# Expert-choice tail: all five chunks summed in PSUM with split one-hot products, and stores that add to a pre-filled output

## What is computed

```python
def expert_choice_ffn(h, w_router, w_gate_up, w_down):
    cap = CAP_FACTOR * N // N_EXPERTS
    aff = jax.nn.softmax((h @ w_router).astype(jnp.float32), axis=-1)
    g, idx = lax.top_k(jnp.swapaxes(aff, 1, 2), cap)
    xs = jax.vmap(lambda hb, ib: hb[ib])(h, idx)
    gu = jnp.einsum('becd,edf->becf', xs, w_gate_up)
    gate, up = jnp.split(gu, 2, axis=-1)
    y = jnp.einsum('becf,efd->becd', jax.nn.silu(gate) * up, w_down) * g[..., None].astype(h.dtype)
    return jax.vmap(lambda ib, yb: jnp.zeros((N, D), yb.dtype).at[ib.reshape(-1)].add(yb.reshape(-1, D)))(idx, y)
...
    ff = expert_choice_ffn(modulate(x, shift2, scale2), w_router, w_gate_up, w_down)
    x = layer_norm(ALPHA * x + gate2 * ff, ln2_g, ln2_b)
```

## Time and profile before

| what | us |
|---|---|
| median of the runs | 950.67 |
| the profiled execution, its own time | 954.81 |
| its span | 953.0 |
| TensorE busy | 880.7 (92%) |
| VectorE busy | 772.8 (81%) |
| ScalarE busy | 574.2 (60%) |
| GpSimd busy | 158.0 (17%) |
| DMA, mean over the span | 285 GB/s |

### The profile page before, as it was taken

How to read it: one execution, slowest core, us unless ns; L and a number is a source line. 1 busy time by engine, 2 the same in 40 slices (tenths; PEclk the granted TensorE clock), 3 DMA queues, 4 the chain that set the end, 5 groups by cost and what they waited for, 6 DMA issues and landing times.

```text
span 953.0 us, 11594 instructions
## 1 busy us (share of the span) xinstructions
PE 880.7 (92%) x4615; PEld 600.9 (63%) x4615; DVE 772.8 (81%) x797; ACT 574.2 (60%) x588; POOL 158.0 (17%) x105
## 2 busy tenths in 40 slices
PE   2899999899999966999999999999999999999982
PEld 0389978256678843666666666666666666666651
DVE  2777736678779876889988988998998998999857
ACT  1345266735751343776776777777777777777732
POOL 1000300110011024103203303302321330320210
PEclk9899999989999986999999999999999999999996
DMA  8920500753048296999999999999999999999525
GB/s 282 396 119 1 205 1 1 291 128 114 2 169 329 100 366 263 355 419 389 416 393 391 411 390 389 400 396 379 384 413 383 379 403 392 372 398 375 181 58 190
DMA packets 57165, 272.08 MB, mean 285 GB/s; under 512 B 6772, under 2 KB 7016, under 8 KB 40728
## 3 DMA queue, kind: packets, MB, share of 16 engines
q1 hardware_dynamic: 48552, 243.81, 65.7%
q0 software_dynamic: 7120, 22.29, 8.5%
q10 hardware_dynamic: 1440, 5.24, 1.4%
HBM read 258.05 MB, written 13.28 MB: 285 GB/s over the span
## 4 chain that ended last, share of the span: by engine, by line
PE 85%; DVE 7%; DMA 4%; ACT 2%; issue 1%; SPq 0%; POOL 0%; DVEq 0%; ACTq 0%
PE PS L903 24%; PE PS L904 24%; PE PS L905 24%; DMA ring<-in_w_mod 3%; PE PS L1067 2%; PE PS L1051 1%; PE PS L918 1%; PE PS L1021 1%; PE PS L1090 1%; PE PS L1222 1%; PE PS L1209 1%; PE PS L1145 1%; DVE xf L1799 1%; DVE smin L1536 1%; ACT prob L710 1%
## 5 line engine op out<-in xcount | busy, mean ns | idle before, releaser
L1716 DVE TENSOR_TENSOR Wl<-wr,Wh 128x2048 fp32r<-128x2048 f32 x190 | 432.6, 2290 | 51.3 <-ACT Wh L821 51.3
L821 ACT ACTIVATE Wh<-wr 128x2048 fp32r<-128x2048 f32 x192 | 367.4, 1915 | 69.1 <-PE PS L905 69.0
L903 PE MATMUL PS<-Wh,Xh 128*80 128x512 f32 x512 | 203.1, 397 | 1.5 <-DVE Xl L1721 0.8
L905 PE MATMUL PS<-Wl,Xh 128*80 128x512 f32 x512 | 201.5, 394 | 0.0
L904 PE MATMUL PS<-Wh,Xl 128*80 128x512 f32 x512 | 201.4, 393 | 0.0
L538 POOL DMA_INDIRECT acc_scratch<-ysc,idx_u x16 | 81.0, 5062 | 428.4 <-DVE ysc L1747 418.7
L905 PEld LDWEIGHTS PS<-Wl,Xh 128*80 128x80 f32 x512 | 76.0, 148 | 42.4 <-issue 0.5
L903 PEld LDWEIGHTS PS<-Wh,Xh 128*80 128x80 f32 x512 | 76.0, 148 | 42.1 <-issue 1.6
L903 PE MATMUL PS<-Wh,HTh 128*80 128x512 f32 x256 | 101.6, 397 | 0.0
L904 PEld LDWEIGHTS PS<-Wh,Xl 128*80 128x80 f32 x512 | 76.1, 149 | 39.5 <-issue 0.4
L904 PE MATMUL PS<-Wh,HTl 128*80 128x512 f32 x256 | 100.4, 392 | 0.0
(11 more groups left out here) (288 smaller groups left out, 1193.6 us busy)
## 6 DMA issues: line engine op xcount, KB each, us to landing
wr<-in_w_gate_up SPq DMA_DIRECT2D x128, 1024.0 KB, 10.1
wr<-in_w_down SPq DMA_DIRECT2D x64, 1024.0 KB, 9.4
ring<-in_w_mod SPq DMA_DIRECT2D x24, 1024.0 KB, 8.9
xt<-in_x_sample ACTq DMA_DIRECT2D x8, 512.0 KB, 7.8
ring<-in_w_in SPq DMA_DIRECT2D x4, 1024.0 KB, 13.4
ring<-in_w_out SPq DMA_DIRECT2D x4, 1024.0 KB, 10.7
w_qkv<-in_w_in SPq DMA_DIRECT2D x4, 768.0 KB, 10.2
h_scratch<-h POOLq DMA_DIRECT2D x5, 512.0 KB, 4.8
```

Of the source, the lines that this page charges most:

```text
L821: act.activation(Wh[n % NWH][:], wr[s][:], ACT.Copy).then_inc(W_hi, 1)
L903: pe.matmul(out, w[0], x[0], start=first, stop=False)
L905: return pe.matmul(out, w[0], x[1], start=False, stop=last)
L1716: dve.tensor_tensor(Wl[s][:], wr[s][:], Wh[n % NWH][:].bitcast(F32), ALU.subtract).then_inc(W_lo, 1)
```

## The change

`FIN_PS` is gone; all five chunks are summed in PSUM, in the banks of `FIN_BANK`, and chunk 4 reuses chunk 0's (it waits for `z_ok`). Expert 15 isn't scattered. Its rows, and for chunk 0 also expert 14's, go through one-hot matrices in single-pass products: ScalarE rounds `ysc` to `yh`, VectorE subtracts for `yl`. Chunk 0 is loaded once scatter 13 is done, chunks 1 to 4 once scatter 14 is; scatter 14 waits until chunk 0 has been read. `FIN_ACT` is chunk 3 alone, read from PSUM. For the sample chunks VectorE makes the centring pass and the reciprocal only, ScalarE makes the multiplication (`scaled`), and the offset `ln2b` is written to all of `y_sample` during expert 3's gate/up slots by four plain stores of GpSimd, so that the last stores, now GpSimd's, add the scaled rows to it in DRAM. The prompt chunk keeps both passes on VectorE and its store on SyncE. At the start the constants' semaphore `const_in` is merged into `rows_in`, and `pads_ok` and `hout` are dropped; where ScalarE and TensorE waited for 9 of `rows_in` they wait for 10.

```diff
@@ -89,7 +89,7 @@
 W_LO_AT = {14: 0, 15: 1}
 K_OUT = (0, 1, 2, 4, 5, 6, 7, 3)
 MOD4_AT = (2, 2, 2, 2, 3, 3, 3, 3)
-FIN_PS, FIN_ACT = (0, 1), (3, 4)
+FIN_BANK, FIN_ACT = (4, 2, 6, 0, 4), 3
 OUT_ORDER = (PC,) + tuple(range(PC))
 W_POOL = 2
 N_HOLD = 8
@@ -262,7 +262,9 @@
     assert XF_SLOT + 3 <= NSLOT
     xf = at("xf", [P, CH, D], Dz + 8192 * XF_SLOT)
     iota = at("iota", [SL, NT], Fz)
-    hot = at("hot", [SL, NT], Fz + 4096)
+    hot = [at("hot0", [SL, P], Fz + 8192, F32R), at("hot1", [SL, NT], Fz + 4096, F32R)]
+    yh = [at("yh0", [SL, D], Cz + 12288, F32R), at("yh1", [SL, D], Dz + 8192 * XF_SLOT + 20480, F32R)]
+    yl = [at("yl0", [SL, D], Cz + 16384, F32R), at("yl1", [SL, D], Fz + 10752, F32R)]
     ln2g = at("ln2g", [P, D], Fz + 32768)
     ln2b = at("ln2b", [P, D], Fz + 36864)
     G2 = at("G2", [SL, D], Cz)
@@ -412,15 +415,14 @@
         sp.wait_ge(x_t, 2 * (NE - 1))
         sp.dma_start(iota[:], t["consts"][0:SL, P + 256:]).then_inc(misc_in, 16)
         sp.wait_ge(W_used, GU0[NE - 1] + 6)
-        sp.wait_ge(scattered, 16 * (NE - 1))
+        sp.wait_ge(scattered, 16 * (NE - 2))
         for c in range(CH):
-            if c == len(FIN_PS):
-                sp.wait_ge(scattered, 16 * NE)
+            if c == 1:
+                sp.wait_ge(scattered, 16 * (NE - 1))
             sp.dma_start(xf[:, c, :], acc_dram[c * P:(c + 1) * P, :]).then_inc(acc_in[c], 16)
-        for c in range(CH):
-            sp.wait_ge(y_out, c + 1)
-            sp.dma_start(y_s[:, c, :] if c < PC else t["y_prompt"][0], xf[:, c, :]).then_inc(stored, 16)
-        sp.wait_ge(stored, 16 * CH)
+        sp.wait_ge(prompt_ok, 1)
+        sp.dma_start(t["y_prompt"][0], xf[:, PC, :]).then_inc(acc_in[PC], 16)
+        sp.wait_ge(acc_in[PC], 32)
 
 
     @block.gpsimd
@@ -529,12 +531,11 @@
 
         def scatter(e):
 
-            pool.wait_ge(y_ok, e + 1 if e < NE - 1 else NE + 1)
+            pool.wait_ge(y_ok, e + 1)
             if e:
                 pool.wait_ge(scattered, 16 * e)
-            if e == NE - 1:
-                for c in FIN_PS:
-                    pool.wait_ge(acc_in[c], 16)
+            if e == NE - 2:
+                pool.wait_ge(acc_in[0], 16)
             pool.indirect_dma_start(acc_dram, bass.IndirectOffsetOnAxis(ap=idx_u[:, e:e + 1], axis=0), ysc[e % 2][:], None,
                                     compute_op=ALU.add).then_inc(scattered, 16)
 
@@ -562,10 +563,17 @@
                 gather(e + 2)
             if e:
                 scatter(e - 1)
-        scatter(NE - 1)
+            if e == 2:
+                pool.wait_ge(ln2_in, 32)
+                for c in range(PC):
+                    pool.dma_start(y_s[:, c, :], ln2b[:]).then_inc(stored, 16)
+        pool.wait_ge(stored, 16 * (2 + PC))
+        for c in range(PC):
+            pool.wait_ge(y_out, c + 1)
+            pool.dma_start(y_s[:, c, :], xf[:, c, :], accum_op=ALU.add).then_inc(stored, 16)
+        pool.wait_ge(stored, 16 * (2 + 2 * PC))
         pool.wait_ge(pool_out, 32)
-        pool.wait_ge(hout, 32)
-
+        
     def x_bank(e, h):
 
         return bank(7 if (e, h) == (0, 1) else 6, 0, 4 * SL)
@@ -872,28 +879,34 @@
             ins.then_inc(act_seq, 1)
             act.wait_ge(act_seq, steps[0])
 
-        def std3(c):
-            act.wait_ge(var3_ok, c + 1)
+        act.wait_ge(hrow_ok, rows_of(NE))
+        act.wait_ge(y_ok, NE - 1)
+        act.activation(yh[0][:], ysc[0][:], ACT.Copy).then_inc(yh_ok, 1)
+        for h in range(2):
+            act.wait_ge(y_ok, NE + h)
+            act.activation(yh[1][:, 512 * h:512 * h + 512], ysc[1][:, 512 * h:512 * h + 512], ACT.Copy).then_inc(yh_ok, 1)
+
+        def std3(c, n):
+            act.wait_ge(var3_ok, n)
             act.activation(nmr[:, c:c + 1], mv[:, c, 1:2], ACT.Sqrt, bias=epsc[:, 0:1]).then_inc(std3_ok, 1)
 
-        def row_sum(c, i):
-            act.wait_ge(acc_in[c], 16)
-            step(act.activation(xt[:, 3, :], xf[:, c, :], ACT.Copy, accum_out=fin[:, 0, i:i + 1]))
-            step(act.activation(nmr[:, c:c + 1], fin[:, 0, i:i + 1], ACT.Copy, scale=-1.0 / D))
-
-        def row_std(c, i):
-            step(act.activation(xt[:, 3, :], xf[:, c, :], ACT.Square, bias=nmr[:, c:c + 1], accum_out=fin[:, 1, i:i + 1]))
-            act.activation(fin[:, 0, i:i + 1], fin[:, 1, i:i + 1], ACT.Sqrt, bias=epsc[:, 0:1],
-                           scale=1.0 / D).then_inc(std3_ok, 1)
-
-        act.wait_ge(hrow_ok, rows_of(NE))
-        std3(0)
-        std3(1)
-        row_sum(3, 0)
-        std3(2)
-        row_std(3, 0)
-        row_sum(4, 1)
-        row_std(4, 1)
+        def scaled(c):
+            act.wait_ge(z_ok, c + 1)
+            act.activation(xf[:, c, :], xf[:, c, :], ACT.Copy, scale=rstd[:, c:c + 1]).then_inc(y_out, 1)
+
+        std3(0, 1)
+        scaled(0)
+        std3(1, 2)
+        scaled(1)
+        std3(2, 3)
+        act.wait_ge(fin_ps, 2 * FIN_ACT + 2)
+        step(act.activation(xt[:, 3, :], PS[:, 512 * FIN_BANK[FIN_ACT]:512 * FIN_BANK[FIN_ACT] + D], ACT.Copy, accum_out=fin[:, 0, 0:1]))
+        step(act.activation(nmr[:, FIN_ACT:FIN_ACT + 1], fin[:, 0, 0:1], ACT.Copy, scale=-1.0 / D))
+        step(act.activation(xt[:, 4, :], xt[:, 3, :], ACT.Square, bias=nmr[:, FIN_ACT:FIN_ACT + 1], accum_out=fin[:, 1, 0:1]))
+        act.activation(fin[:, 0, 0:1], fin[:, 1, 0:1], ACT.Sqrt, bias=epsc[:, 0:1], scale=1.0 / D).then_inc(std3_ok, 1)
+        scaled(2)
+        std3(4, 4)
+        scaled(3)
 
 
     @block.tensor
@@ -1266,15 +1278,23 @@
 
         pe.wait_ge(hrow_ok, rows_of(NE))
         pe.wait_ge(y_ok, NE - 1)
-        for c in FIN_PS:
+        pe.wait_ge(hot_ok, 2)
+        for c in range(CH):
             pe.wait_ge(acc_in[c], 16)
+            if c == PC:
+                pe.wait_ge(z_ok, 1)
+            out = [bank(FIN_BANK[c] + h) for h in range(2)]
             for h in range(2):
-                pe.matmul(bank(4 - 2 * c + h), ident, xf[:, c, 512 * h:512 * h + 512], start=True, stop=False)
+                pe.matmul(out[h], ident, xf[:, c, 512 * h:512 * h + 512], start=True, stop=False)
             if c == 0:
-                pe.wait_ge(hot_ok, 1)
+                pe.wait_ge(yl_ok, 1)
+                for h in range(2):
+                    pe.matmul(out[h], hot[0][:], yh[0][:, 512 * h:512 * h + 512], start=False, stop=False)
+                    pe.matmul(out[h], hot[0][:], yl[0][:, 512 * h:512 * h + 512], start=False, stop=False)
             for h in range(2):
-                pe.wait_ge(y_ok, NE + h)
-                pe.matmul(bank(4 - 2 * c + h), hot[:, c * P:(c + 1) * P], ysc[(NE - 1) % 2][:, 512 * h:512 * h + 512],
+                pe.wait_ge(yl_ok, 2 + h)
+                pe.matmul(out[h], hot[1][:, c * P:(c + 1) * P], yh[1][:, 512 * h:512 * h + 512], start=False, stop=False)
+                pe.matmul(out[h], hot[1][:, c * P:(c + 1) * P], yl[1][:, 512 * h:512 * h + 512],
                           start=False, stop=True).then_inc(fin_ps, 1)
 
 
@@ -1706,8 +1726,8 @@
         dve.tensor_tensor(idx_u[0:CAP_S, :], diff, ib, ALU.add).then_inc(slot_ok, 1)
         dve.tensor_tensor(g_slot[0:CAP_S, :], va, vb, ALU.max)
         dve.tensor_copy(g_slot[CAP_S:SL, :], vp)
-        dve.tensor_tensor(idx_last[0:CAP_S, :], diff[:, NE - 1:NE], ib[:, NE - 1:NE], ALU.add)
-        dve.tensor_copy(idx_last[CAP_S:SL, :], ip[:, NE - 1:NE]).then_inc(slot_ok, 1)
+        dve.tensor_tensor(idx_last[0:CAP_S, :], diff[:, NE - 2:NE], ib[:, NE - 2:NE], ALU.add)
+        dve.tensor_copy(idx_last[CAP_S:SL, :], ip[:, NE - 2:NE]).then_inc(slot_ok, 1)
 
         def split_lo_slot(n):
 
@@ -1751,7 +1771,15 @@
 
             dve.wait_ge(misc_in, 32)
             dve.wait_ge(x_t, 2 * NE)
-            dve.tensor_scalar(hot[:], iota[:], idx_last[:, 0:1], None, ALU.is_equal).then_inc(hot_ok, 1)
+            for i in range(2):
+                dve.tensor_scalar(hot[i][:], iota[:, 0:P if i == 0 else NT], idx_last[:, i:i + 1], None, ALU.is_equal).then_inc(hot_ok, 1)
+
+        def y_lo(i, h, lo, hi):
+
+            dve.wait_ge(yh_ok, i + h + 1)
+            if i == 0:
+                dve.wait_ge(ht_ps, 2 * NE)
+            dve.tensor_tensor(yl[i][:, lo:hi], ysc[i][:, lo:hi], yh[i][:, lo:hi].bitcast(F32), ALU.subtract).then_inc(yl_ok, 1)
 
         x_lo(0, 0)
         x_lo(0, 1)
@@ -1760,6 +1788,8 @@
         for n in range(W_POOL, len(ORDER) + LEAD + 3):
             if n < len(ORDER):
                 split_lo_slot(n)
+            if n == len(ORDER):
+                y_lo(0, 0, 0, D)
             for e in range(NE):
                 for h in range(2):
                     if e + 1 < NE and n == GU0[e] + X_AT[h] + LEAD:
@@ -1776,27 +1806,39 @@
 
 
         dve.wait_ge(ln2_in, 32)
-        for c in range(CH):
-            x = xf[:, c, :]
-            src = PS[:, 2048 - 1024 * c:3072 - 1024 * c] if c in FIN_PS else x
-            if c not in FIN_ACT:
-                if c not in FIN_PS:
-                    dve.wait_ge(acc_in[c], 16)
-                for h in range(2):
```

(68 more changed lines are left out.)

## The result

| | before | the change |
|---|---|---|
| median | 950.67 us | 955.28 us |
| ratio, 95% interval | | 1.0047 (1.0028 to 1.0065) |
| profiled execution: own time | 954.81 us | 955.28 us |
| its span | 953.0 us | 953.5 us |
| end of the split products | 922.30 us | 919.48 us |

The change is slower by 0.47%, 2.7 to 6.2 us by the interval. The forecast was 947.5 in a range of 943.3 to 951.0: wrong in sign and outside its range. One of the change's five executions ran at a mean granted clock of 0.62 and took 1380.85 us; the ratios leave out such slow ones, which the kernel before has too.

A forecast was written before the change was run, and what follows sets the result against it. It took the tail behind the split products as what could move, with VectorE the chain up to 949.95 us. Its terms ended the span at 949.9 against 953.0, -3.1 us off the 950.67 median: 947.5, range 943.3 to 951.0.

The forecast's parts named there:

- the 0.4: At the very end: 0.4 us from the last store's landing to the end of the span, giving 949.9.
- last landing: In the tail: the prompt's plain store lands last, at 949.5 us, behind store 3 at 948.2.
- the starved middle: Rival, around expert 4: the fill leaves TensorE standing still for up to 5.2 us; 952.7 us, chance 0.15.
- scatter 14's issue lengthened: Ahead of the tail: VectorE's subtraction delays GpSimd's descriptor writing for scatter 14 by 1.1 us, bounds 0 and 1.2.
- store 3 issued: In the tail: GpSimd's adding store of chunk 3 goes out at 941.05 us, after ScalarE scales it.
- prompt's store issued: In the tail: the prompt chunk's plain store goes out at 942.6 us, once VectorE has scaled chunk 4.
- an adding packet: In the last stores: a 4 KB packet of an adding store takes 312 to 328 ns, a plain one 160.
- an adding store alone, issue to landing: In the last stores: one adding store by itself takes 6.0 us, bounds 3.8 and 6.2.
- The fill: During expert 3: four plain stores to y_sample, 5.2 us of DMA time, costed at nothing behind a weights' lead of 10.
- The half clock: Rival, before chunk 1: TensorE falls to half clock in a 1.3 us pause, costing 3.4 us; 950.9 us, chance 0.10.
- The plain price: Rival, last stores: adding stores cost what plain ones do, so the prompt path ends it; 943.3 us, chance 0.15.
- the second rival's: Rival, last stores: adding stores run at the scatter's mean rate, 466 ns a packet, +1.3 us; 948.8 us, chance 0.12.

The follow-up runs named there:

- j: Run g with adding stores for chunks 0, 1 and 2 in place of 0 and 1: median 947.61 us, ratio 0.995 against the kernel before.
- a: The change with SyncE, not GpSimd, waiting for the landing of the adding stores: median 951.98 us, ratio 1.0008 against the kernel before.
- d: The change without the four plain stores that write ln2b to y_sample during expert 3: median 955.26 us, ratio 1.0034 against the kernel before.
- c: The change with GpSimd's last four stores plain, so the offset is left out: median 952.89 us, ratio 1.0012 against the kernel before.
- e: Run a with VectorE's subtraction for expert 14's low part moved behind expert 15's evacuation: median 952.69 us, ratio 1.001 against the kernel before.
- h: Run g with VectorE's subtraction for expert 14's low part moved behind expert 15's evacuation: median 944.78 us, ratio 0.9928 against the kernel before.
- g: Run f with fill and adding stores for chunks 0 and 1 only, SyncE waiting for every landing: median 945.21 us, ratio 0.9938 against the kernel before.
- i: Run a with plain stores in place of adding ones, so the offset is left out: median 948.91 us, ratio 0.9961 against the kernel before.
- b: The kernel before, with GpSimd also waiting at its end for SyncE's five plain stores: median 959.3 us, ratio 1.0074.
- f: The change without fill and adding stores; VectorE makes both passes for all five chunks, SyncE stores them: median 947.33 us, ratio 0.9952 against the kernel before.

## Why the prediction was wrong

**The step that failed** is the last one of the sum: "With the 0.4 between the last landing (949.98 + 2.6) and the end that is 949.9". I took the 0.4 from a program in which SyncE was the last to wait and carried it into one in which GpSimd is. Measured in its place: 0.2 from GpSimd's last landing, 945.3, to the drain, 7.7 of drain, 0.2 to the end. The prediction went through the release of every store and never asked which engine stands last in line and what it still has to do. The evidence was in the trace of before, as a record of 8.64 us behind GpSimd's last instruction, in no view of busy time. No rival named it; the starved middle, the only one on the slow side, was another mechanism.

**The rest of the sum held.** Measured from the end of the split products:

| step | predicted | measured |
|---|---|---|
| scatter 14's issue lengthened | 1.1 | 1.35 (5.00 against 3.65) |
| first load to landing | 4.02 | 3.3 |
| store 3 issued | 18.75 | 18.45 |
| prompt's store issued | 20.3 | 19.57 |
| an adding packet | 312 to 328 ns | 333 to 338 ns |
| an adding store alone, issue to landing | 6.0 | 5.3 (j, chunk 2) |
| last landing | 27.2 | 25.8 to 26.1 |
| landing to end of span | 0.4 | 7.9 |

The last landing is 25.8 us for GpSimd's stores and 26.1 for the prompt's, 1.1 us early, and what follows it is 7.5 too long: together the 6.4 us that were to be found. With 0.4 in the last row the tail would have been 26.5 us, 4.2 under before. No run shows that with all four adding stores. In the nearest, a, SyncE has seen every landing 26.1 us behind the split products, but the drain, begun at the last issue, ends 3.7 us later.

**The fill** was rightly costed at nothing (d), but of the lead of "10" us that was to hide it, 3.6 remain. Each of its four issues took 1.05 to 1.12 us, not 0.55. Its rival was right about the crowding; those 3.6 us kept it from deciding.

**The half clock** was rightly kept as a rival: it did not occur in the change's profile, with a pause of 0.6 us on TensorE, and did in c's with one of 2.3. What it costs the median can't be told from zero (a against e).

**The descriptors.** VectorE's subtraction has both inputs in SBUF and writes SBUF; moving it away shortened the scatter's issue by 1.1 us, from 5.00 to 3.86 (e, and h against g). The Trainium skill, page SBUF — State Buffer, section SBUF: two separate sides, infers that such an instruction spares descriptor writing. Here it does not, and the measurement decides.

**The plain price** (15%) is out: the packets cost double a plain one's 160 ns. The Trainium skill, page DMA: Bandwidth & Descriptors, section on the anatomy of a GpSimd DMA, fits 2.0 us plus bytes over 436 GB/s, by which I had estimated 3.2 us for such a store. An adding store alone took 5.3 (j), and the change's last one 7.4, issued 1.5 us behind another; a plain one issued so took 3.0 (i). The prediction calls the end by this estimate "the second rival's"; it is that of the first, the plain price. And the 3.8 us that it took as the least for a plain store were no bound.

## What to carry to other kernels

Ask of every edit which engine makes the last wait of the program and what it has to do after it: here one wait for landings on GpSimd, in addition to SyncE's, cost 7 to 8 us in a kernel where nothing else changed (b). Let SyncE wait for the landings at the end, and give GpSimd its last store some 9.3 us before the end, 11.6 with two adding ones 1.5 us apart; behind a long issue, as of a scatter, 7.3 us count from where the issue ends (f). A change of two halves is to be timed in halves: the sums in PSUM were worth 4.2 us (f), the adding stores perhaps 2.1 more for the first two chunks (g), and with all four the gain was gone (a, 1.0008 against f's 0.9952).

## What the runs showed of the hardware

GpSimd's drain at the end of its program, 7.2 to 7.7 us behind a wait in four kernels, with adding stores, plain ones or only a scatter, was the surprise, and with it that the barrier's wait stands in the profile under another engine's name. What GpSimd does in that time no run shows; the drain at the start of the program takes it 0.19 us. At its issue an adding store occupies GpSimd for 0.83 to 0.96 us and a plain one in the same place for 0.53 to 0.61 (c, i), but each of the fill's plain ones took 1.05 to 1.12. An adding store's 4 KB packets take 333 to 338 ns against 160.
